# Down weights of experts 7 to 27 requested by ScalarE behind its copies, gate and up weights by SyncE alone

## The reference, cut to what matters

```python
def hier_moe(h, w_rg, b_rg, w_re, b_re, w_gate, w_up, w_down):
    ...                                         # router: top-1 group of 4, top-2 of its 8 experts
    a = jnp.einsum('bld,edf->blef', h, w_gate)  # w_gate, w_up: 32 x 1024 x 256
    u = jnp.einsum('bld,edf->blef', h, w_up)
    act = jax.nn.silu(a) * u * combine.astype(h.dtype)[..., None]
    return jnp.einsum('blef,efd->bld', act, w_down)   # w_down: 32 x 256 x 1024
```

## Time and profile before

| | |
|---|---|
| median of 3 runs | 717.39 us (715.14 to 719.43) |
| the profiled execution | 712.98 us, of which the span 710.9 us |
| TensorE matmul busy | 632.5 us, 89% |
| ScalarE busy | 150.9 us, 21% |
| DMA | 242.91 MB, mean 342 GB/s |

### The profile page before, as it was taken

How to read it: one execution, slowest core, us unless ns; L and a number is a source line. 1 busy time by engine, 2 the same in 40 slices (tenths; PEclk the granted TensorE clock), 3 DMA queues, 4 the chain that set the end, 5 groups by cost and what they waited for, 6 DMA issues and landing times.

```text
span 710.9 us, 14200 instructions
## 1 busy us (share of the span) xinstructions
PE 632.5 (89%) x5287; PEld 461.8 (65%) x5287; DVE 279.3 (39%) x1532; ACT 150.9 (21%) x429; POOL 103.0 (14%) x138
## 2 busy tenths in 40 slices
PE   6999999799999999997969999987897996769684
PEld 4888888677888876773636877666553653444431
DVE  3002864997878877610000212435224221111114
ACT  3334323333325323300010000221101110101012
POOL 1465305440010223100000000011100110000001
PEclk9999999999999999998899999999999999898898
DMA  9937998999998999989999999659999999999991
GB/s 306 300 131 264 347 362 285 305 350 383 375 344 262 403 396 320 406 309 401 358 400 350 375 396 399 249 213 363 336 393 400 377 388 401 393 394 394 417 351 69
DMA packets 94904, 242.91 MB, mean 342 GB/s; under 512 B 8834, under 2 KB 54530, under 8 KB 86514
## 3 DMA queue, kind: packets, MB, share of 16 engines
q1 hardware_dynamic: 58050, 193.51, 71.9%
q10 hardware_dynamic: 31200, 31.39, 13.4%
q0 software_dynamic: 5584, 17.08, 7.1%
HBM read 234.88 MB, written 9.11 MB: 343 GB/s over the span
## 4 chain that ended last, share of the span: by engine, by line
PE 61%; DMA 17%; DVE 10%; SPq 7%; issue 3%; ACT 1%; POOL 0%; DVEq 0%; ACTq 0%; POOLq 0%
PE zps L930 36%; DMA ring_all<-in_w_up 7%; PE nps L1234 6%; SPq L436 3%; DVE kall L1433 3%; PE zps L1257 3%; DMA ring_all<-in_w_ret_o 3%; DMA out<-xs 2%; PE nps L900 2%; DMA ring_all<-in_cache_v 2%; DMA xs<-in_state_ret 2%; PE bps L1272 1%; SPq L430 1%; PE zps L1223 1%; SPq L431 1%
## 5 line engine op out<-in xcount | busy, mean ns | idle before, releaser
L930 PE MATMUL zps<-hT,ring_all 128*128 128x264 f32 x1152 | 271.7, 391 | 1.0 <-DVE hT L1614 1.0
L930 PEld LDWEIGHTS zps<-hT,ring_all 128*128 128x128 f32 x1152 | 216.7, 192 | 43.4 <-issue 3.3
L1433 DVE CUSTOM_DVE_ANT_0 kall<-kall,qb 128x128 f32<-128x128 f32 x512 | 130.3, 320 | 64.0 <-DMA kall<-in_cache_k 61.4
L930 PE MATMUL zps<-headT,ring_all 128*128 128x264 f32 x256 | 62.5, 407 | 4.3 <-DMA ring_all<-in_w_ret_o 3.9
L613 POOL DMA_INDIRECT rows_b<-h_rows,tidx_i x16 | 15.2, 952 | 329.5 <-DVEq L1700 180.0
L930 PEld LDWEIGHTS zps<-headT,ring_all 128*128 128x128 f32 x256 | 50.9, 201 | 15.6 <-issue 5.6
L1775 DVE TENSOR_TENSOR qdT<-qdT,nps 128x64 f32<-128x64 f32 x32 | 7.1, 221 | 99.4 <-ACT qdT L833 98.5
L1433 DVE DVE_READ_ACCUMULATOR2_ANT scores<- 128x1 f32 x512 | 40.7, 79 | 0.0
L833 ACT ACTIVATE qdT<-nps 128x64 f32<-128x64 f32 x32 | 7.2, 224 | 141.5 <-PE nps L1234 141.5
L1093 PE MATMUL nps<-ring_all,zret 128*32 128x256 f32 x448 | 29.7, 401 | 6.7 <-DMA ring_all<-in_cache_v 6.7
L1234 PE MATMUL nps<-ring_all,gain 128*32 128x128 f32 x640 | 23.7, 307 | 12.1 <-DMA ring_all<-in_w_up 11.2
(11 more groups left out here) (373 smaller groups left out, 836.5 us busy)
## 6 DMA issues: line engine op xcount, KB each, us to landing
kall<-in_cache_k SPq DMA_DIRECT2D x64, 512.0 KB, 6.8
ring_all<-in_cache_v SPq DMA_DIRECT2D x56, 512.0 KB, 7.6
ring_all<-in_w_in ACTq DMA_DIRECT2D x26, 1024.0 KB, 10.5
ring_all<-in_w_gate SPq DMA_DIRECT2D x10, 1024.0 KB, 21.1
ring_all<-in_w_up SPq DMA_DIRECT2D x10, 1024.0 KB, 22.7
ring_all<-in_w_down SPq DMA_DIRECT2D x8, 1024.0 KB, 11.4
ring_all<-in_w_in SPq DMA_DIRECT2D x6, 1024.0 KB, 13.2
kall<-in_w_gate SPq DMA_DIRECT2D x5, 1024.0 KB
```

The source lines that it names most:

```text
L930: mm = pe.matmul(zps[m % 2][:, 0:T], w[:, k, P * fb:P * (fb + 1)], rhs[:, k, :], start=(k == 0), stop=(k == KT - 1))
L1433: ins = v.tensor_tensor_reduce(kh, kh, qb[b % 2][:, P * h:P * (h + 1)], 1.0, 0.0, ALU.mult, ALU.add, scores[:, pg, AH * b + h:AH * b + h + 1])
```

## The change

SyncE's loop keeps only the gate and up weights. ScalarE asks for the down weights of experts 7 to 27, in its own queue, in bursts of four: at expert 4q + 6, behind its copy of the second half of quad q, it asks for experts 4q + 7 to 4q + 10 (at q = 5 for 27 alone). The copy itself waits for quad q's second half of down products. The sizes, the places and the semaphores of the transfers are the same, and so are the last four experts' halves on SyncE.

```diff
@@ block.sync @@
-            def next_down(e):
-                sp.wait_ge(e_D, 2 * ((e - SETS) // 4 + 1))
-                down_in(e % SETS, e)
-
-            downs = SETS
             for e in range(SETS, NE):
                 sp.wait_ge(e_GU, e + 1 - SETS)
                 gate_up_in(e % SETS, e)
-                while downs <= min(e - (4 if e < 16 else 2), NE - 5):
-                    next_down(downs)
-                    downs += 1
-            for e in range(downs, NE - 4):
-                next_down(e)
             sp.wait_ge(e_D, 2 * ((NE - 2 - SETS) // 4 + 1))
@@ block.scalar @@
+            def next_downs(q):
+
+                for e in range(4 * q + SETS, min(4 * q + SETS + 4, NE - 4)):
+                    act.dma_start(down_w[e % SETS].rearrange("p (f n) -> p f n", f=FB),
+                                  w_down[0, e].rearrange("(f p) n -> p f n", p=P)).then_inc(d_in[e % SETS], 16)
+
             for e in range(NE):
                 silu(e % 2, e + 1)
                 if 5 <= e < NE - 3 and e % 4 in (1, 2):
                     y_copy(zps[1], slice(0, P), e % 4 - 1, 2 * (e // 4 - 1) + e % 4)
+                    if e % 4 == 2:
+                        next_downs(e // 4 - 1)
```

## The result

The changed kernel took 724.61 us (723.09 to 726.36) against 717.39: ratio 1.0106, 95% interval 1.0061 to 1.015. Measured again beside the experiments it took 727.43 against 715.45: 1.0171 (1.0136 to 1.0206). So it is slower, by 7 to 12 us. Its profiled execution took 724.61 us, span 722.5, 11.6 more than before. In two experiments (gate and up weights in pieces of 4 KB, and the burst behind the copies) one execution each took some 3466 us; it is in their medians, and out of their ratios.

The account below looks back on a forecast made before the run. The prediction took the end to hang on expert 29's weights and down weights 27, in a stage with saturated DMA engines. Late down weights added 10 us to 717.39, giving 727.4 us, range 715 to 734.

Parts of the forecast that it names:

- The bound: End of the expert stage: it hangs on when the products at 673.70 us can start, on expert 29's weights and down weights 27.
- The share: Two competing queues, served packet for packet: down weights get one third of the bandwidth, 8.3 us per transfer; 27 lands late, +10 us.
- The sum: Whole kernel: +10 us on the median of 717.39 us, giving 727.4 us.
- the last halves: End of SyncE's queue, 2 KB rows: 4 KB down rows win two thirds, so the last 1 MB takes 4.2 us instead of 8.3.
- the hole: Stretch 510 to 515 us at 234 GB/s: it fills with 0.83 MB, worth 0 to 2.1 us.
- ScalarE's issue time: Four 1 MB requests a quad ahead of silu: 2.2 us, taken to cost 0, with 12 us a quad as far end.
- The second case: Rival, down weights in time: every quad's weights land before their need, +0.5 us, 717.9 us; chance 0.26.

Follow-up runs that it names:

- e9_changed: The changed kernel itself measured once more, in more rounds, against the kernel before: 727.43 us, ratio 1.0171.

## Why the prediction was right

*The bound* was read rightly: time hangs on when quad 6's down products start. In all fourteen profiled executions the span ends 37.0 to 39.9 us behind that start, which itself lies between 673.3 and 704.5 us.

*The share.* One third and 8.3 us for each down transfer were forecast from queues with rows of 4 KB against 1 KB. One third it was, packet for packet. From the first request (509.79 us) to the landing of 27 (682.93) it took 173.1 us for 21, 8.24 each on average. Down weights 15, 19, 23 and 27 came at 589, 622, 654 and 683 us (forecast 587, 620, 653, 683.5); the waits were 8.7, 10.2, 8.6 and 6.1 us (forecast 10, 12, 12 and 9.5, the last for TensorE ready at 674; it was ready at 677).

*The sum.* +10 us forecast; in the profiled executions 9.2 at the start of quad 6's products plus 2.3 for the fallen clock, 11.6 together, and 7.2 and 12.0 in the two comparisons. The clock was no term of the forecast. Executions also differ by their start: in the changed kernel's trace the first gate and up products come 0.9 us earlier than in the trace before.

*Wrong in a step:* the last halves, in rows of 2 KB, were to lose against 4 KB. They did not. From 670 to 682 us:

```profile
q1 hardware_dynamic: 1083, 3.40, 72.0%
q10 hardware_dynamic: 351, 1.32, 27.5%
```

Three packets to one over the stretch. Its last 4 us hold only the tail of 27 (571 to 55), but from 674 to 678 us it is already 335 to 143, 1.02 MB to 0.54: the down weights kept their third of the bytes and did not get two thirds. That the time of 27 was met all the same is in part luck. The first nine transfers took 8.8 us each (15 came 2 us later than forecast, from a request 2.7 us earlier); the last four took 7.2 us each, 4.3 us less together than 8.3 each would make, where 4.2 were forecast for the end. The reason lies elsewhere: from 655 to 675 us the engines moved 410 to 419 GB/s instead of the 389 that were taken for the whole stage, and no packet of GpSimd's gathers was among them. The share had not changed. From 654 to 670 us:

```profile
q1 hardware_dynamic: 597, 4.32, 65.0%
q10 hardware_dynamic: 599, 2.31, 36.1%
```

In the second profiled execution of this kernel (the run e9_changed) the first request came at 512.99 us, 15 at 591.5 and 27 at 684.63, with the same slow start and quick end.

*Mis-sized:* the hole. Its 0.83 MB were moved as said, but alone they gave no 2.1 us.

*ScalarE's issue time* at 0 was right here: ScalarE's copies waited 13.0 us in all behind its requests, and without any hold, in the run with single requests, the time is the same. It is not small by nature, as the run with 2 KB pieces shows. *The second case*, down weights in time, is what the kernel becomes with equal pieces: forecast +0.5 us, measured 1.0027 (-0.1 to +3.9 us).

## What to carry to other kernels

When a transfer moves to a second queue, its place in the order is given up for a share, and the share goes by packet size: compare the pieces of both queues, multiply out when the k-th transfer lands, and hold that against each need. Late weights inside a stream-bound stage may cost nothing; ask which wait is the last that nothing behind it can make good. An engine that computes should not issue more packets than its queue takes at once: with 2 KB pieces ScalarE's computing stood still behind them, and the kernel lost 4%.

## What the runs showed of the hardware

- Two full queues were served packet for packet for 8 KB against 4 KB (653 to 655), 4 KB against 4 KB (1038 to 995), and 8 KB against 2 KB (626 to 671). Where SyncE's queue passed from 8 KB to the halves in 2 KB, against 4 KB on ScalarE, it was 335 to 143 in 4 us. Why is open.
- The rate of a full stage was not one number: 410 to 419 GB/s from 655 to 675 us, where no gather ran, and dips to 316 to 354 GB/s within some 10 us behind gathers, both at a full share. That the gathers make the dips was not tested.
- ScalarE stood 5.57 us in the fourth request of the third burst, with about 5 MB in 4 KB pieces outstanding (an estimate: 11 requests made, 6 landed at 8.8 us each). In 2 KB pieces it stood already in the fifth to eighth request of 512 KB (5.37 and 11.54 us for two each). As an estimate from the two, a queue has room for 1100 to 1300 packets; this was not measured by itself.
